# A two-block fp32 network on one core: filler matmuls, wide-then-narrow weight passes, and another way from the experts to the dense layers

## What is computed

```python
def first_block(x, c, ...):
    ...                                        # modulation, retention, attention, x = x + gate_m * rmsnorm(mixed)
    h = rmsnorm(x, g_pre_ffn[l]) * (1.0 + scale_f) + shift_f
    moe = expert_choice_moe(h, w_router[l], w_gate_e[l], w_up_e[l], w_down_e[l])
    x = x + gate_f * rmsnorm(moe, g_post_ffn[l])
    return x

def swiglu_ffn(h, w_up, w_down):
    u = h @ w_up
    a, b = jnp.split(u, 2, axis=-1)
    return (jax.nn.silu(a) * b) @ w_down

def second_block(x, ...):
    for l in range(DEPTH_2):                   # two layers
        x = x + 0.5 * swiglu_ffn(rmsnorm_2(x, norm_ffn1[l]), ffn1_w_up[l], ffn1_w_down[l])
        x = x + hybrid_mixer(rmsnorm_2(x, norm_mix[l]), w_in[l], ...)
        x = x + 0.5 * swiglu_ffn(rmsnorm_2(x, norm_ffn2[l]), ffn2_w_up[l], ffn2_w_down[l])
    return rmsnorm_2(x, final_norm)
```

## Time and profile before

| | us |
|---|---|
| median of three runs | 2248.8 |
| the three runs | 2248.8, 2243.2, 2249.28 |
| the profiled execution | 2244.06 |
| its span in the trace | 2242.2 |
| PE busy in the span | 1929.2 (86%) |
| DVE, ACT busy | 1055.1 (47%), 690.3 (31%) |
| DMA traffic | 658.09 MB |

### The profile page before, as it was taken

How to read it: one execution, slowest core, us unless ns; L and a number is a source line. 1 busy time by engine, 2 the same in 40 slices (tenths; PEclk the granted TensorE clock), 3 DMA queues, 4 the chain that set the end, 5 groups by cost and what they waited for, 6 DMA issues and landing times.

```text
span 2242.2 us, 29455 instructions
## 1 busy us (share of the span) xinstructions
PE 1929.2 (86%) x12503; PEld 1387.7 (62%) x12503; DVE 1055.1 (47%) x1254; ACT 690.3 (31%) x775; POOL 39.3 (2%) x25
## 2 busy tenths in 40 slices
PE   7999766666676666676799999999999999999998
PEld 5775222122222222222488899998888889999887
DVE  5773000000000000000387678877778767887776
ACT  4543000000000000000244448453444444845344
POOL 0100000000000000000000002000000000200000
PEclk9999888888887878888899999999999999999999
DMA  9789999999999999999855755555575575555554
GB/s 369 265 345 399 427 428 428 427 429 427 429 428 428 429 427 429 428 428 430 329 188 153 204 179 194 171 203 185 148 228 188 153 205 178 197 170 203 185 146 134
DMA packets 232934, 658.09 MB, mean 294 GB/s; under 512 B 6356, under 2 KB 121476, under 8 KB 208260
## 3 DMA queue, kind: packets, MB, share of 16 engines
q1 hardware_dynamic: 232836, 656.67, 76.4%
HBM read 655.60 MB, written 1.05 MB: 293 GB/s over the span
## 4 chain that ended last, share of the span: by engine, by line
PE 65%; DMA 33%; ACT 1%; DVE 1%; issue 1%; SPq 0%; DVEq 0%; ACTq 0%
DMA ring<-in_w_down_e_dram 24%; PE psum L1295 13%; PE psum L1399 7%; PE psum L1296 7%; PE psum L1317 5%; PE psum L1318 5%; PE psum L1319 5%; PE psum L1400 4%; DMA ring<-in_w_gate_e_dram 4%; DMA ring<-in_w_up_e_dram 4%; PE psum L1195 3%; PE psum L1217 2%; PE psum L1244 2%; PE psum L1175 2%; DMA ring<-in_w_ada_dram 1%; PE psum L1366 1%
## 5 line engine op out<-in xcount | busy, mean ns | idle before, releaser
L2383 DVE TENSOR_TENSOR ring_r<-ring,ring_r 128x2048 fp32r<-128x2048 f32 (+2 forms) x182 | 453.2, 2521 | 87.1 <-ACT ring_r L1747 86.9
L1747 ACT CAST ring_r<-ring 128x2048 fp32r<-128x2048 f32 (+2 forms) x180 | 360.2, 2041 | 304.3 <-PE psum L1400 115.9
L1295 PE MATMUL psum<-work_r,ring_r 128*128 128x512 f32 x1280 | 448.3, 396 | 0.7 <-DVE ring_r L2383 0.7
L1296 PE MATMUL psum<-work_r,ring_r 128*128 128x256 f32 x1280 | 357.2, 279 | 0.0
L1295 PEld LDWEIGHTS psum<-work_r,ring_r 128*128 128x128 f32 x1280 | 240.3, 188 | 58.9 <-issue 1.0
L1195 PE MATMUL psum<-ring,work 128*32 128x512 f32 x1280 | 189.0, 719 | 100.9 <-DMA ring<-in_w_up_e_dram 75.2
L1317 PE MATMUL psum<-work_r,ring_r 128*128 128x256 f32 x928 | 264.2, 285 | 0.0
L1318 PE MATMUL psum<-work_r,ring_r 128*128 128x256 f32 x928 | 262.5, 283 | 0.0
L1319 PE MATMUL psum<-work_r,ring_r 128*128 128x256 f32 x928 | 262.1, 282 | 0.0
L1399 PE MATMUL psum<-work_r,ring_r 128*128 128x512 f32 x704 | 246.6, 396 | 0.0
L2357 DVE TENSOR_SCALAR work<-psum,wide_cols,mod 128x32 f32<-128x32 f32 x128 | 33.9, 306 | 440.6 <-PE psum L1175 440.6
(11 more groups left out here) (335 smaller groups left out, 2118.5 us busy)
## 6 DMA issues: line engine op xcount, KB each, us to landing
ring<-in_w_down_e_dram SPq DMA_DIRECT2D x47, 2048.0 KB, 40.4
ring<-in_w_gate_e_dram SPq DMA_DIRECT2D x42, 2048.0 KB, 40.7
ring<-in_ffn_w_up_dram SPq DMA_DIRECT2D x41, 2048.0 KB, 7.9
ring<-in_w_up_e_dram SPq DMA_DIRECT2D x38, 2048.0 KB, 40.5
work<-in_w_up_e_dram SPq DMA_DIRECT2D x26, 2048.0 KB, 40.6
ring<-in_w_in_dram SPq DMA_DIRECT2D x25, 2048.0 KB, 8.0
work<-in_w_gate_e_dram SPq DMA_DIRECT2D x22, 2048.0 KB, 40.5
ring<-in_ffn_w_down_dram SPq DMA_DIRECT2D x32, 1408.0 KB, 7.1
```

What stands on the lines that cost most here:

```text
L1295: pe.matmul(dst, w_hi[:, k, cols], h_both(k), start=(k == 0), stop=False)
L1296: mm = pe.matmul(dst[:, 0:S], w_lo[:, k, cols], h_hi_[:, S * k:S * (k + 1)], start=False, stop=(k == KD - 1))
L1747: act.copy(hi_unit(name, unit), raw_unit(name, unit)).then_inc(hi_ready, 1)
L2383: dve.tensor_tensor(lo_unit(name, unit), raw_unit(name, unit), hi_unit(name, unit).bitcast(F32), ALU.subtract).then_inc(lo_ready, 1)
```

## The change

1. **Fillers.** `warm` is defined ahead; PE runs 10 fillers before the first transpose, 8 and 14 between the halves of the two weight pairs of the head (before: none and 5) and 3 after the first pair. In the third expert of each turn 5, 7, 10 and 2 fillers stand behind the four down tiles.
2. **Order.** `paired_passes` runs all eight wide matmuls of a block and then all eight narrow ones. The down products run 22 wide and then 22 narrow, the first output block in runs of two.
3. **The expert's result** leaves PSUM in two halves, one by ACT and one by DVE; PE waits for the second half only before the fifth of its eight matmuls, and signals each two of them.
4. **The norm at the turn.** Each bank is squared when its two matmuls are done, DVE adds two pairs of chunks, and six matmuls of 256 columns with a full matrix of 1/1024 give the mean square of each token on all partitions. ACT takes the root of a row of 256, DVE inverts the row. The spread and the copy are gone.
5. **The first layer tile** comes in two transfers of four rows each. DVE casts the first half, ACT the second; DVE makes the low part in four pieces, the last of them between the chunks. 28 fillers instead of 42.
6. **Chunks.** DVE scales two chunks at a time instead of four. PE takes the first tile with k outermost, in four banks at once, and the mean square before the last k.

```diff
@@ sync: first layer tile
+                        if name == ("upa", 0, 0):
+                            view = slot_view(name, KD, 512)
+                            sp.dma_start(view[:, 0:4], w[:, 0:4, at:at + 512]).then_inc(first_rows_loaded, 16)
+                            parts = [(view[:, 4:8], w[:, 4:8, at:at + 512])]
@@ tensor: head
             pe.wait_ge(consts_ready, 1)
+            warm(10)
...
                 half_modulation(i + 1, 0).then_inc(tile_done[i], 1)
-                if i:
-                    warm(5)
+                warm(14 if i else 8)
...
                 modulation_columns(i)
-            warm(10)
+                warm(10 if i else 3)
@@ tensor: expert
                     down_products(q)
-
-                pe.wait_ge(y_ready, e + 2)
+                    if j == TOGETHER:
+                        warm((5, 7, 10, 2)[q], 0)
+
                 for c in range(KD):
+                    if c == 0:
+                        pe.wait_ge(y_ready, e + 2)
+                    if c == KD // 2:
+                        pe.wait_ge(y_high_ready, e + 2)
                     mm = pe.matmul(moe_acc[:, c, :], y_part[:, P * c:P * (c + 1)], gT_,
                                    start=(j == 0 and c % 2 == 0), stop=True, skip_group_check=True)
-                mm.then_inc(moe_done, 1)
+                    if c % 2:
+                        mm.then_inc(moe_done, 1)
@@ tensor: turn
-            square_sums(sq_ready, 1, 0, ms_done)
-            spread_columns(rstd_ready, 1, bank[0], TT, rstd_spread)
+            for c, first in ((0, True), (1, False), (4, False), (5, False), (6, False), (7, False)):
+                if c == 0:
+                    pe.wait_ge(sq_added, 1)
+                elif c in (4, 6):
+                    pe.wait_ge(sq_ready, c // 2 + 1)
+                mm = pe.matmul(bank[0][:, 0:S], mean_d[:].broadcast_to([P, P]), h[:, c, :], start=first, stop=(c == KD - 1))
+            mm.then_inc(ms_done, 1)
...
-            pe.wait_ge(lo_ready, splits.ready(("upa", 0, 0), 0, 0))
-            keep_warm(bank[2], hi_unit(("upa", 0, 0), 0), 3 * WARM)
+            pe.wait_ge(head_lo, KD + 2)
+            keep_warm(bank[2], hi_unit(("upa", 0, 0), 0), 2 * WARM)
@@ tensor: paired_passes
                         for k in range(KD):
                             pe.matmul(dst, w_hi[:, k, cols], h_both(k), start=(k == 0), stop=False)
+                        for k in range(KD):
                             mm = pe.matmul(dst[:, 0:S], w_lo[:, k, cols], h_hi_[:, S * k:S * (k + 1)], start=False,
                                            stop=(k == KD - 1))
@@ tensor: first_pairs
+                    if l == 0 and i == 0:
+                        for k in range(KD):
+                            if k % 2 == 0:
+                                pe.wait_ge(head_lo, KD + k // 2 + 1)
+                            pe.wait_ge(h_lo_ready, k + 1)
+                            if k == KD - 1:
+                                mean_square(1, 0)
+                            for q in range(2):
...
+                                for b in range(2):
...
@@ tensor: down products
+                        run = 2 if c == 0 else FK
+                        for first in range(0, FK, run):
+                            ks = range(first, first + run)
+                            for k in ks:
+                                if c == 0:
+                                    u_chunk(k)
+                                pe.matmul(dst, w_hi[:, k, :], u_both(k), start=(k == 0), stop=False)
+                            for k in ks:
+                                mm = pe.matmul(dst[:, 0:S], w_lo[:, k, :], u_hi[:, S * k:S * (k + 1)], start=False,
+                                               stop=(k == FK - 1))
@@ scalar
-                act.copy(y_part, two_banks[1]).then_inc(y_ready, 1)
+                act.copy(y_part[:, 0:512], bank[2]).then_inc(y_ready, 1)
...
-            act.wait_ge(moe_done, E)
             for b in range(4):
+                act.wait_ge(moe_done, 4 * (E - 1) + b + 1)
                 act.activation(h[:, 2 * b:2 * b + 2, :], moe_acc[:, 2 * b:2 * b + 2, :], ACT.Square).then_inc(sq_ready, 1)
-            root(0, 1)
...
+            for part in (slice(2048, 3072), slice(3072, 4096)):
+                act.copy(ring_r[:, s, part], ring[:, ring_plan.slot(name), part]).then_inc(head_hi, 1)
+            act.wait_ge(ms_done, 1)
+            act.activation(rstd_row[:], bank[0][:, 0:S], ACT.Sqrt, bias=EPS).then_inc(std_ready, 1)
@@ vector
+                dve.tensor_copy(y_part[:, 512:1024], bank[3]).then_inc(y_high_ready, 1)
...
+            def first_low_part(q):
+                part = slice(1024 * q, 1024 * (q + 1))
+                dve.tensor_tensor(ring_r[:, at, part], ring[:, at, part], ring_r[:, s, part].bitcast(F32),
+                                  ALU.subtract).then_inc(head_lo, 1)
...
+            dve.wait_ge(first_rows_loaded, 16)
+            step(dve.tensor_copy(ring_r[:, s, 0:2048], ring[:, at, 0:2048]))
+            first_low_part(0)
+            dve.wait_ge(sq_ready, 2)
+            dve.tensor_tensor(h[:, 0:2, :], h[:, 0:2, :], h[:, 2:4, :], ALU.add).then_inc(sq_added, 1)
+            first_low_part(1)
+            dve.wait_ge(head_hi, KD + 1)
+            first_low_part(2)
+            dve.wait_ge(std_ready, TT + 1)
+            step(dve.reciprocal(rstd_row[:], rstd_row[:]))
...
-            for b in range(2):
...
+            for b in range(4):
...
+                step(dve.tensor_tensor(pair, moe_acc[:, 2 * b:2 * b + 2, :],
+                                       rstd_row[:].unsqueeze(1).broadcast_to([P, 2, S]), ALU.mult))
...
+                if b == 2:
+                    dve.wait_ge(head_hi, KD + 2)
+                    first_low_part(3)
```

101 lines of the change are left out of this document (41 added, 60 removed).

## The result

| | before | after |
|---|---|---|
| median, us | 2245.49 (19 runs) | 2249.05 (19 runs) |
| from, to | 2243.2, 2250.67 | 2245.69, 2253.66 |
| profiled execution, its span | 2244.06, 2242.2 | 2253.66, 2251.9 |

The ratio is 1.0020, with an interval of 1.0012 to 1.0028: the change makes the kernel slower, by 2.7 to 6.3 us (the two medians alone lie 3.6 us apart). The forecast was 5.5 us less. The profiled execution of after is the slowest of its runs, so of the 9.6 us between the two profiles only some 4.5 belong to the change.

A forecast was written before the change was run, and what follows sets the result against it. It took the weight stream to bound the experts and PE's matmul pace the layers, with the turn's chain between. Head 0, order -4.5 and turn -1.0 us took 2248.8 to 2243.3 us; eight-in-ten range 2237 to 2252 us.

The forecast's parts named there:

- covered by the weight stream: Expert loop: fillers of the first four expert turns and the split copy hide behind the weight DMA, 0 us.
- Behind 28.09 us nothing is different: Head: after the matmul that the DMA releases at 28.09 us, the added head fillers change nothing.
- The base of the forecast: Whole kernel: the starting time of 2248.8 us from which the gain of 5.5 us was taken.
- The head: 0 to +0.6 us: Head: added fillers end before the second pair's second half lands, 0 us taken, up to +0.6 us if late.
- the worse of the two cases: Head: with the clock still down, the fillers end some 0.6 us too late.
- The order: -4.5 us: Layers' feed-forwards: wide and narrow matmuls in separate runs cost the first slightly more, the second less; -4.5 us in sum.
- my two values: Feed-forwards: a pair taken apart costs 346.7 ns, or 348.9 ns at the slower narrow pace.
- The two isolated matmuls: Feed-forwards: the skill's rule, columns over 2.4 GHz plus 2.5 ns, gives 324.9 ns a pair in any order.
- first feed-forward fast, second slow: Layers: alternating pairs take 346.5 ns in the first feed-forward and 353.5 ns in the second, 992 pairs each.
- The turn: -1.0 us: Between experts and layers: first scaling 3.8 us earlier, but DVE's longer chain leaves 1.0 us at the end of the squares.
- the slower rival: Feed-forwards and turn: slow pace everywhere, +6.9 us, and half clock after PE's waits costing 1.4 us; 2256.1 us, chance 0.09.
- the slow pace everywhere: Layers: 353.5 ns a pair holds in all four feed-forwards, +6.9 us; part of the slower rival, chance 0.09.

The follow-up runs named there:

- e7: The change with POOL's gate product waiting for DVE's low part and 6 wide loop fillers instead of 24 narrow: 2242.26 us, 0.9976 of the kernel before.
- e17: The change with POOL's gate product waiting for DVE's low part and the old head fillers: 2242.02 us, 0.9981 of the kernel before.
- e2: The change with the alternating order put back in half-tile passes and down products: 2253.44 us, 1.0028 of the kernel before.
- e5: The kernel before with only POOL's gate product made to wait for DVE's low part: 2247.93 us, 0.9990 of the kernel before.
- e10: The kernel before with POOL's gate product waiting for DVE's low part and the change's 24 loop fillers: 2243.69 us, 1.0001 of the kernel before.
- e12: The kernel of e8 with the alternating order put back: 2244.03 us, 0.9989 of the kernel before.
- e14: The kernel before with POOL's gate product waiting for DVE's low part and 25 loop fillers: 2242.43 us, 0.9988 of the kernel before.
- e18: The kernel before with POOL's gate product waiting for DVE's low part, 24 loop fillers and the change's head fillers: 2251.16 us, 1.0016 of the kernel before.
- e16: The change itself, unaltered, timed again beside other runs: 2252.14 us, 1.0027 of the kernel before.
- e1: The kernel before with the new order alone: 2244.63 us, 0.9985 of the kernel before.
- e6: The kernel before with the new order and POOL's gate product waiting for DVE's low part: 2242.86 us, 0.9971 of the kernel before.
- e3: The change with POOL's gate product made to wait for DVE's low part: 2249.48 us, 1.0008 of the kernel before.
- e4: The change without the fillers in the expert loop: 2245.32 us, 0.9992 of the kernel before.
- e9: The kernel of e7 with 18 one-column matmuls added behind the wide loop fillers: 2252.23 us, 1.0027 of the kernel before.
- e13: The change with POOL's gate product waiting for DVE's low part and 23 loop fillers instead of 24: 2248.53 us, 1.0009 of the kernel before.
- e8: The kernel of e7 with 7 and 11 fillers added in PE's two waits of the first layer tile: 2240.17 us, 0.9958 of the kernel before.
- e15: The kernel of e8 timed a second time, beside the change: 2241.13 us, 0.9976 of the kernel before.
- e11: The kernel of e8 with the head of the kernel before: 2242.19 us, 0.9988 of the kernel before.

## Why the prediction was wrong

**The bounds** were read rightly: the experts go by the weight stream, the layers by PE's pace. What failed is the sentence that the fillers of the expert turns are "covered by the weight stream", and with it the head's "Behind 28.09 us nothing is different". I asked only for the time that the fillers take on PE, and that time is indeed covered (e7). Their code is not: it travels through the same DMA engines as the weights. The term was 0 and is +7.8 us (882.9 against 875.1). Without it (e17) the change is at 0.9981, faster by 4.3 us (1.3 to 7.2). That is near the forecast of 5.5, but in part by luck: e17 has the old head and the toss settled, and the settled toss, which the forecast did not have, is worth 1.74 us in each layer that POOL would have won. Why 36 packets cost 7.8 us is open: at 427 GB/s their 0.59 MB are 1.4 us. What the traces show is that the DMA engines never ran out of work until the last tiles (share 1.00), so it was not PE that gave its slots back late, and that they then finished unevenly (0.58 in the last 6 us, against 0.97).

That 2249.05 us lies between 2237 and 2252 us is no success. The base of the forecast, 2248.8 us from three runs, was 3.3 us above the median of 19, and the change goes the other way.

**The head: 0 to +0.6 us.** The row moved within these bounds. PE in the head of after, for the earlier trace rows:

```profile
21.59 3.30 PE L868 MATMUL psum<-ring,work 128*32 128x512 f32 x16 [0.52 <-DMA ring<-in_w_ada_dram]
24.81 3.66 PE L812 MATMUL psum<-ident 128*128 128x128 f32 x28
28.41 1.92 PE L868 MATMUL psum<-ring,work 128*32 128x512 f32 x16
```

No DMA releases the last row now, and it comes 0.32 us later: the fillers ran at half clock at first, as in the worse of the two cases. Whether the kernel pays for it is open. The first expert's product comes at 214.8 to 222.5 us in the eight traces with the old head and at 214.2 to 218.4 us in the twelve with the new one, which is not later.

**The order: -4.5 us.** The mechanism was right and the sum too high. The first and third feed-forward should have lost 0.2 to 2.4 us and the others gained 4.6 to 6.7. The table gives +1.1 us for the third (+0.92 and +0.15) and -2.3 to -2.5 for the second and fourth. With the third's loss for the first as well, whose up products the clock disturbs, that is +2.1 - 4.8 = -2.7 us. The pace in runs is 349 ns a pair, not the 348 between my two values: from start to start, a wide matmul in a run of eight takes 230.7 ns in the mean and not 226.7, a narrow one 118.9 and not 120 to 122 (in the down products, with runs of 22, a pair takes 61.05 us / 176 = 347 ns). (The two isolated matmuls of the prediction's next paragraph add up to 325.0 ns, not 324.9; nothing rests on it.) The other error was to take "first feed-forward fast, second slow" for a property of the kernel. In seven traces with the alternation (before, e2, e5, e10, e12, e14, e18) the last three feed-forwards were slow 9 times of 21, in four patterns. Against that mean (up 117.5, down 61.4 us) the new order's 117.4 and 61.05 are worth about 1.7 us. The times gave 0.01 or 0.08% (e16 or after against e2), 0.15% (e1) and 0.19% (e6 against e5), so 0 to 4 us.

**The turn: -1.0 us.** Each step came nearly as written: the last down product 1.92 us, the first scaling 3.58 us earlier (forecast 3.8), the end of the squares 0.57 us earlier (forecast 1.0), and PE waits for the low part again (1132.78). Then the clock took it back in most traces. It fell to 0.50 in the first tile's last matmuls in after, e16 and e17, and in e2, e3, e4, e7, e9 and e13 in the second tile. From the last down tile to the first down product of the layers, in the new order: 144.8 us with the old turn (e1, e6), 144.2 in after and e17, 145.7 in e3, e7 and e13, 146.9 in e16. A block at half clock costs 4.27 - 2.87 = 1.40 us (e7 against e8), which is the 1.4 us of the slower rival, whose other half (the slow pace everywhere) did not come. With the fillers of e8 and e15 the clock stays up, and it is 144.2 both times, 0.6 us gained.

The granted clock falls after PE's waits of 2.15 to 3.0 us in these traces and, with fillers in them (e8, e11, e12, e15), does not. This agrees with the Trainium skill, page "TensorE: Matmul & The Clock Gate", section "Why this matters for your kernels", on idle gaps between bursts.

**What no step had:** the meeting of DVE and POOL in the mixers. It costs 1.74 us in each layer in which POOL is first. The profile of after holds it twice and that of before not at all, so 3.2 us of the 9.6 between the two profiles (179.34 + 179.12 against twice 177.62). Whether it weighs equally on both in the medians is not shown: of the free meetings POOL won one of four in kernels made from before (before, e1) and five of eight in those made from the change (after, e2, e4, e16), which is too few to tell.

**The sum of the measured terms:** +7.8 (fetches), -2.7 (order), -0.6 to +2.1 (turn), +0.3 (head, by its row alone) give +4.8 to +7.5 us. Measured are +4.5 (2.7 to 6.3) and, beside e15, +6.1 (3.8 to 8.1).

**Better than both** is the kernel of e8 and e15: the change with six wide fillers in the loop, fillers in PE's two waits of the turn, and POOL behind DVE's low part. It takes 0.9958 and 0.9976 of the kernel before, 5 to 9 us less, and 11 us less than the change beside it (e16).

## What to carry to other kernels

Filler instructions cost code as well as time: look at the packets of the instruction queue before and after, and build fillers from few wide matmuls, above all in and ahead of a loop that shares the DMA engines with a weight stream. Very narrow ones save little: seven of one column took 1.6 us (e9), where ten of 128 columns take 2.5 us. Read a pace or a waiting order from more than one execution before you call it a property of the kernel; where two engines start within 20 or 30 ns of each other and exclude each other, write the order down. A wait that a shorter chain leaves to PE needs fillers in the same edit, or the clock takes the gain back.
